# Identity products on TensorE at seven stage boundaries of a two-block transformer kernel

## The reference

```python
h = modulate(rmsnorm(x, g_norm1), sh1, sc1)            # normalise, then a product with weights
o = concat([o_mla, o_ret]) @ w_out
x = x + gt1 * o
x = x + gt2 * conv_ffn(modulate(rmsnorm(x, g_norm2), sh2, sc2), w_up, conv_w, conv_b, w_down)
x = rmsnorm(x, g_final)
# second block: mod = silu(c) @ ada_w + ada_b gives shift, scale and gate of each stage
y = gmlp_mixer(modulate(rms_norm(x, g), shift, scale), ...)     # then swiglu
k, v, dcum = shared_kv(x, ...)
y = fox_mixer(modulate(rms_norm(x, g), shift, scale), ...)      # then swiglu
x = x + gate * rms_norm(y, post_g)
```

## Time and profile before

| | |
|---|---|
| median of the runs | 1320.44 us (1318.26 to 1327.59) |
| span of the profiled execution | 1323.4 us |
| PE busy | 1181.9 us, 89% of the span |
| PE weight loads (PEld) busy | 1011.9 us, 76% |
| DVE busy | 796.9 us, 60% |
| ACT busy | 583.0 us, 44% |
| chain that ended last | PE 75%, DVE 13%, ACT 6%, issue 4%, DMA 1% |

### The profile page before, as it was taken

One profiled execution on the slowest core, in us unless ns is written; L12 is line 12 of the kernel. 1 busy time (PEld: TensorE's weight loads), 2 busy tenths in 40 slices (PEclk: granted clock), 3 DMA queues, 4 the chain that ended last, 5 costly groups with the idle time before them and its releaser, 6 DMA issues.

```text
span 1323.4 us, 17991 instructions
## 1 busy us (share of the span) xinstructions
PE 1181.9 (89%) x7087; PEld 1011.9 (76%) x7087; DVE 796.9 (60%) x774; ACT 583.0 (44%) x802; POOL 219.9 (17%) x169
## 2 busy tenths in 40 slices
PE   6699989698999996979969999987989877999996
PEld 1288746578999885778849999865867765999985
DVE  0444447665766777897853449575588757444443
ACT  0632443445666435343354444244444435444432
POOL 2000510102555201020001223100102000122300
PEclk9999999888999997999979999997899977999998
DMA  8755434153555896966844559693695414466540
GB/s 317 270 191 184 159 112 144 40 190 108 182 188 191 291 342 209 377 211 231 320 148 141 179 181 342 257 347 112 227 323 184 158 64 159 127 190 183 185 173 32
DMA packets 124094, 263.68 MB, mean 199 GB/s; under 512 B 8281, under 2 KB 76321, under 8 KB 113793
## 3 DMA queue, kind: packets, MB, share of 16 engines
q1 hardware_dynamic: 120081, 246.16, 53.7%
q0 software_dynamic: 2800, 8.29, 2.2%
q10 hardware_dynamic: 1152, 8.39, 1.6%
HBM read 261.76 MB, written 1.05 MB: 199 GB/s over the span
## 4 chain that ended last, share of the span: by engine, by line
PE 75%; DVE 13%; ACT 6%; issue 4%; DMA 1%; SPq 0%; ACTq 0%; DVEq 0%
PE ps L1446 21%; PE ps L1448 21%; PE ps L1447 21%; DVE acc L537 3%; PE ps L1528 2%; DVE wl L525 2%; ACT wh L1047 2%; ACT hraw L1084 1%; ACT xn L1058 1%; PE ps L1501 1%; PE ps L1649 1%; PE ps L1619 1%; DVE x L626 1%; PE ps L1467 1%; PE ps L1633 1%
## 5 line engine op out<-in xcount | busy, mean ns | idle before, releaser
L525 DVE TENSOR_TENSOR wl<-raw,wh 128x2048 fp32r<-128x2048 f32 (+1 forms) x159 | 361.8, 2277 | 332.9 <-ACT wh L1047 332.9
L1047 ACT ACTIVATE wh<-raw 128x2048 fp32r<-128x2048 f32 (+1 forms) x159 | 301.4, 1896 | 431.3 <-PE ps L1448 431.3
L1446 PE MATMUL ps<-hh,wh 128*128 128x256 f32 (+1 forms) x1192 | 337.4, 283 | 10.5 <-DVE hl L606 5.2
L1447 PE MATMUL ps<-hl,wh 128*128 128x256 f32 (+1 forms) x1192 | 336.6, 282 | 0.0
L1448 PE MATMUL ps<-hh,wl 128*128 128x256 f32 (+1 forms) x1192 | 336.4, 282 | 0.0
L1446 PEld LDWEIGHTS ps<-hh,wh 128*128 128x128 f32 (+1 forms) x1192 | 225.8, 189 | 13.5 <-issue 8.9
L1447 PEld LDWEIGHTS ps<-hl,wh 128*128 128x128 f32 (+1 forms) x1192 | 225.7, 189 | 0.2
L1448 PEld LDWEIGHTS ps<-hh,wl 128*128 128x128 f32 (+1 forms) x1192 | 225.6, 189 | 0.2
L537 DVE SCALAR_TENSOR_TENSOR acc<-au,cs,acc 128x2048 f32<-128x2048 f32 x72 | 172.7, 2399 | 4.8 <-DMA au<-in_ada_w_dram 4.6
L1446 PE MATMUL ps<-wh,hh 128*128 128x512 f32 (+1 forms) x352 | 140.8, 400 | 20.9 <-DVE cl L606 10.8
L2035 POOL TENSOR_TENSOR gl<-hid,gh 128x256 f32 (+1 forms) x66 | 93.2, 1413 | 332.1 <-ACT gh L1287 332.1
(11 more groups left out here) (288 smaller groups left out, 1412.3 us busy)
## 6 DMA issues: line engine op xcount, KB each, us to landing
au<-in_ada_w_dram SPq DMA_DIRECT2D x48, 1024.0 KB, 7.0
raw<-in_ffn_w_gu_dram SPq DMA_DIRECT2D x88, 512.0 KB, 4.6
raw<-in_w_up_dram SPq DMA_DIRECT2D x44, 512.0 KB, 4.7
raw<-in_ffn_w_down_dram SPq DMA_DIRECT2D x44, 512.0 KB, 4.2
au<-in_w_ada_dram SPq DMA_DIRECT2D x16, 1024.0 KB, 5.7
raw<-in_a_w_in_dram SPq DMA_DIRECT2D x32, 512.0 KB, 5.5
raw<-in_w_down_dram SPq DMA_DIRECT2D x22, 512.0 KB, 4.4
raw<-in_w_in_dram SPq DMA_DIRECT2D x16, 512.0 KB, 4.7
```

The lines of the kernel that those rows point to most:

```text
L525: nc.vector.tensor_tensor(wl[:, s % 2, 0:n], raw[:, u % RAW, 0:n], wh[:, s % 2, 0:n].bitcast(F32), ALU.subtract).then_inc(lo_done, 1)
L1047: nc.scalar.activation(wh[:, s % 2, 0:n], raw[:, u % RAW, 0:n], ACT.Copy).then_inc(hi_done, 1)
L1446: nc.tensor.matmul(to, lh, rh, start=start, stop=False, skip_group_check=True)
L1447: nc.tensor.matmul(to, lh, rl, start=False, stop=False, skip_group_check=True)
```

## The change

A helper `keep_busy(bank, count)` issues `count` float32 matmuls of the 128x128 identity with itself into the first 128 columns of a PSUM bank. `turn` calls it twice: ahead of the wait on `xn_ready`, into the bank that the first transposes overwrite, and behind the transposes, into bank 0. The call ahead stands behind the wait on `ex_taken`. Two lists hold the counts.

```diff
+BUSY_BEFORE = [0, 0, 28, 14, 36, 34, 48, 0, 18, 18]
+BUSY_AFTER = [0, 0, 0, 6, 7, 6, 5, 0, 0, 6]
...
+            def keep_busy(bank, count):
+
+                for _ in range(count):
+                    nc.tensor.matmul(ps[:, bank, 0:P], ident, ident, start=True, stop=True, skip_group_check=True)
+
             def turn(n, src, b0, after=None):

                 if after is not None:

                     pe.wait_ge(ex_taken, EX_BASE[after + 1])
+                keep_busy(b0, BUSY_BEFORE[n])
                 pe.wait_ge(xn_ready, XN_NEED[n])
                 for b in range(4):
                     for q in range(4):
...
                     ins.then_inc(turned, 1)
+                keep_busy(0, BUSY_AFTER[n])
```

## The result

Ten runs after the change have a median of 1333.89 us (1327.68 to 1337.1), ten of before 1323.8 us (1318.26 to 1338.67), the three of the first table among them. The ratio is 1.0072, with a 95% interval of 1.0049 to 1.0095: 0.7% slower, within the 1% named as what a measurement tells, and clear of no change. The profiled execution after has a span of 1332.5 us, 9.1 more than before.

The account below looks back on a forecast made before the run. PE was taken to bound the kernel, with 75% of the chain and waits at seven boundaries. Lateness 21.0 less gains 8.6 gave 12.4 us more: 1320.4 + 12.4 = 1333 us, 0.9% slower; range 1324 to 1341 us at 8 in 10.

Parts of the forecast that it names:

- Where the products start: At four boundaries products start only after the wait on `ex_taken`; transposes were to be 21.0 us late over all boundaries.
- The price of a product: At every boundary, one identity product was taken to cost 0.224 us at full clock and 0.43 us at half clock.
- The restart at half clock: At N_FF0, N_MIX1, N_FF1 and N_FF2 the first 4.2 us of products were to run at half clock (rows: 3.3 to 5.1).
- What comes back: Full clock was to gain 2.8 us in transposes at seven boundaries and 5.8 us in products behind them: 8.6 us.
- The products behind the transposes: The 5 to 7 products in PE's wait for DVE's `hl` were costed at nothing; uncovered, 0.8 us a boundary.
- The median: The base: the profiled execution's 1323.4 us was read as 3.0 us above the runs' median, giving 1320.4 us.
- Transposes keep the clock: Denies a rival: transposes don't hold the clock, costing some 7 us more at up to five boundaries, 1340 us; chance 0.04.
- The mixer swallowed nothing: Denies a rival: DVE sets the pace behind N_MIX1 and its 7.0 us lateness is hidden, 1326 us; chance 0.08.
- the identity costs the full price of its form: Denies a rival: products at a quarter of L1690's time, 0.056 us, so nothing is late, 1312 us; chance 0.03.
- rival 2: Identity products, nearly all zeros, don't hold the clock at any boundary; each then costs 0.43 us, 1367 us; chance 0.07.

## Why the prediction was right, point by point

- **Where the products start.** Right. At N_MIX1 they began when DVE had handed over the modulation (L555 in the waits of after), and the experiments that move one wait (0.9904) or cut the counts (0.9907) turn the sign. Lateness was 19.8 us in all, where I had 21.0.
- **The price of a product.** Right: 0.112 us a record at full clock. At N_MIX1 14 records at half clock (some 0.21 us each) and 58 at full clock give 3.0 + 6.5 = 9.5 of the 9.76 us.
- **The restart at half clock.** The term that was sized worst for single boundaries. I took 4.2 us for all four; it was 3.1 at N_MIX1, 4.0 at N_FF1, 6.1 at N_FF2 and none at N_FF0, where the clock had come back at 295.30, half a microsecond before the first identity product, so that none of them had a part in it. N_FF0 came out 1.7 us below the forecast and N_FF2 2.0 above, and the sum hid it: the sum owes that much to luck. My bounds of 3.3 to 5.1 us were too narrow on both sides.
- **What comes back.** 9.8 us between lateness and net, where I had 8.6. The first bank gives 0.45 us (first product at N_RET 10.42 us after the stage's end for 10.88). N_KV gave 2.4 us, where I had 1.6.
- **The products behind the transposes.** Their cost was right, near nothing; that they gain was not in my sum. They win some 5 us on top of the fill ahead (0.9941 to 0.9904) and 7 us alone. The step "I cost them at nothing" had a cover but left out the gain.
- **The median.** I set the span of the profiled execution, 1323.4 us, against the median of three runs and read it as 3.0 us above. A span lacks 1.8 us that the time of the run has (1332.5 and 1334.3 us for the profiled execution after), so that execution took some 1325.2 us, 1.4 above the median of ten runs, 1323.8. The sum of 12.4 was high by 2.3 (10.1 between the medians; the interval of the ratio leaves 6.5 to 12.6), the base low by 3.4: 1333 for 1333.9 us is partly luck.
- **The rivals.** Transposes keep the clock (run with them as filler). Identity products hold it (N_RET and N_KV at 1.00). The mixer swallowed nothing: N_MIX1's 4.8 us are followed by +0.1 us up to the next boundary. And the identity costs the full price of its form. In rival 2 the figure for N_KV doesn't follow from its own terms: 4.4 us at full clock and 28.4 products at 0.43 us end 4.4 us late and not 3.8, which would make that rival 0.6 us dearer.

What stays open is the spread of single executions. The kernel with only N_RET, N_KV and N_FOX filled has N_MIX1 unchanged, and its first product comes 14.89 us after the stage's end as before. Its 60th product is 2.6 us later, since the clock came back only at 511.54, 5.8 us after the first product, where in the trace of before it was back 1.3 us ahead of it:

```profile
505.00:506.00 1.00, 0.28 (x1) 0.29 (x2) 0.66 (x2) 0.84 (x2) 0.00 (x0) 0.50 1.05 406
...
511.00:512.00 1.00, 1.00 (x5) 0.81 (x4) 0.00 (x0) 0.00 (x0) 0.00 (x0) 0.73 0.00 0
```

So the same code at the same place wins or loses 2.6 us by the moment at which the clock switches. Boundary sums of one trace carry that error, and part of the 20 us between the fastest and slowest run of before may come from it, which was not tested.

## What to carry to other kernels

A filler for a waiting engine must end before what the engine waits for. Size it by the room from its own start, at the clock that it will find there. Ahead of every wait of the boundary the full counts fit but for 1.5 us at N_MIX1 and 0.4 us at N_FOX (0.9904); behind a late wait only 4 to 7 products did, and they won as much (0.9907); what lost time was a count meant for the whole idle time in the small room behind the wait (1.0072). Fill the wait behind as well, since work that gets faster makes the next wait longer. And look for which engine ends the wait: a full clock ahead of that moment was worth 0.05 us at N_FF0.

## What the hardware did that I had not expected

- One-column products kept PE and PEld at 1.00 busy, and the clock fell 2.8 us after the first of them. With 128 columns it stayed at 1.00, through 6.4 us of products at N_RET and 10.9 us at N_KV, and through over 10 us of transposes at N_KV.
- The half clock at a restart lasted from 3.1 to 6.1 us, counted from the first identity product, under the same stream of products.
